# The first layer's shift and scale in two column parts instead of one, in a three-part-precision transformer kernel

## The reference

```python
cond = jax.nn.silu(c)                                   # (1, 1024)
mod = cond @ ada_w[l] + ada_b[l]                        # (1, 3072)
shift, scale, gate = jnp.split(mod, 3, axis=-1)
h = x * (1.0 + scale[:, None, :]) + shift[:, None, :]
proj = h @ w_in                                         # even_mixer: u, v, z_a, x_b, z_b
v = layer_norm(v.reshape(B, S, GMLP_HEADS, GMLP_HEAD_DIM), norm_g, norm_b)
sv = jnp.einsum('hts,bnshd->bnthd', w, v) + bs.T[:, :, None]
```

## Time and profile before

| | us |
|---|---|
| median of 3 runs | 1318.17 (1317.94 to 1319.11) |
| the profiled execution: time | 1319.02 |
| the profiled execution: span | 1317.2 |
| TensorE busy | 1289.7 (98%) |
| VectorE, ScalarE, GpSimd busy | 941.3, 580.2, 357.4 |
| first matmul of any kind | 10.86 |
| first matmul of tile 0 | 34.10 |

### The profile page before, as it was taken

The page is one execution under the profiler, slowest core; times in us unless marked ns, Lnnn a source line. Parts: engine busy times, 40 slices in busy tenths (PEclk is TensorE's granted clock), DMA queues, the critical chain, the costliest instruction groups (busy, mean ns, idle before and its releaser), DMA issues.

```text
span 1317.2 us, 18039 instructions
## 1 busy us (share of the span) xinstructions
PE 1289.7 (98%) x6874; PEld 1106.0 (84%) x6874; DVE 941.3 (71%) x1415; ACT 580.2 (44%) x889; POOL 357.4 (27%) x262
## 2 busy tenths in 40 slices
PE   5999999999999999999999999999999999999997
PEld 5998888778898888888888878888888988888887
DVE  7765654796777558888678888776785577776663
ACT  1422322321264347666422587653452477734441
POOL 1200210055620004655434221122115322221122
PEclk9999999999999999999999999999999999999999
DMA  9565666537725620111234311213533111212111
GB/s 376 171 199 180 187 201 193 158 117 204 234 79 153 174 87 21 41 52 51 88 122 142 112 65 64 96 53 110 154 97 115 65 64 65 95 55 75 64 64 64
DMA packets 35093, 155.18 MB, mean 118 GB/s; under 512 B 6848, under 2 KB 9024, under 8 KB 23744
## 3 DMA queue, kind: packets, MB, share of 16 engines
q1 hardware_dynamic: 35008, 154.04, 36.9%
HBM read 151.92 MB, written 2.10 MB: 117 GB/s over the span
## 4 chain that ended last, share of the span: by engine, by line
PE 88%; DVE 5%; issue 3%; ACT 1%; POOL 1%; DMA 1%; SPq 0%; DVEq 0%; POOLq 0%; ACTq 0%
PE bank L971 25%; PE bank L973 24%; PE bank L972 24%; PE bank L1334 2%; PE bank L1319 1%; PE bank L1338 1%; PE bank L1179 1%; DVE keep L2477 1%; PE bank L1510 1%; PE bank L1537 1%; PE bank L1535 1%; DMA ada_first<-adat 1%; PE bank L1307 1%; PE bank L1306 1%; PE bank L978 1%
## 5 line engine op out<-in xcount | busy, mean ns | idle before, releaser
L971 PE MATMUL bank<-h_lo,w_hi 128*128 128x512 f32 (+1 forms) x1064 | 407.1, 383 | 0.7 <-DVE k_both L2045 0.5
L973 PE MATMUL bank<-h_hi,w_hi 128*128 128x512 f32 (+1 forms) x1064 | 402.5, 378 | 0.0
L972 PE MATMUL bank<-h_hi,w_lo 128*128 128x512 f32 (+1 forms) x1064 | 402.2, 378 | 0.0
L1883 DVE TENSOR_TENSOR w_lo<-w_raw,w_hi 128x2048 fp32r<-128x2048 f32 (+2 forms) x91 | 207.1, 2275 | 75.6 <-ACT w_hi L1557 75.4
L971 PEld LDWEIGHTS bank<-h_lo,w_hi 128*128 128x128 f32 x1064 | 200.2, 188 | 37.6 <-issue 1.8
L973 PEld LDWEIGHTS bank<-h_hi,w_hi 128*128 128x128 f32 x1064 | 200.1, 188 | 37.7
L972 PEld LDWEIGHTS bank<-h_hi,w_lo 128*128 128x128 f32 x1064 | 200.3, 188 | 36.3 <-issue 0.2
L1557 ACT ACTIVATE w_hi<-w_raw 128x2048 fp32r<-128x2048 f32 (+2 forms) x91 | 166.7, 1832 | 89.7 <-PE bank L973 72.9
L1925 DVE SCALAR_TENSOR_TENSOR acc<-ada_raw,cond_four,acc 128x1024 f32<-128x1024 f32 x62 | 87.5, 1411 | 3.9 <-DMA ada_raw<-adat 1.0
L1685 ACT ACTIVATE tmp<-bank 128x512 f32<-128x512 f32 x48 | 28.8, 600 | 112.3 <-PE bank L973 111.1
L2477 DVE TENSOR_TENSOR_SCAN keep<-keep,rmats 128x127 f32<-128x127 f32 (+2 forms) x64 | 57.8, 942 | 1.0
(11 more groups left out here) (359 smaller groups left out, 2688.1 us busy)
## 6 DMA issues: line engine op xcount, KB each, us to landing
w_raw<-wt SPq DMA_DIRECT2D x83, 1024.0 KB, 5.5
ada_raw<-adat SPq DMA_DIRECT2D x256, 128.0 KB, 2.9
ada_first<-adat SPq DMA_DIRECT2D x16, 512.0 KB, 12.2
ada_raw<-adat SPq DMA_DIRECT2D x32, 256.0 KB, 5.7
w_raw<-wt SPq DMA_DIRECT2D x8, 640.0 KB, 3.9
spare_raw<-wt SPq DMA_DIRECT2D x3, 1024.0 KB, 5.1
x<-xt SPq DMA_DIRECT2D x4, 512.0 KB, 15.5
out<-outf SPq DMA_DIRECT2D x16, 128.0 KB, 1.8
```

Source lines behind the costliest of these rows:

```text
L971: pe.matmul(dst, ah, bl, start=start, stop=False, skip_group_check=True)
L972: pe.matmul(dst, al, bh, start=False, stop=False, skip_group_check=True)
L973: return pe.matmul(dst, ah, bh, start=False, stop=stop, skip_group_check=True)
L1883: dve.tensor_tensor(w_lo[wb[T]][:, 0:n], w_raw[wb[T]][:, 0:n], f(w_hi[wb[T]][:, 0:n]), ALU.subtract).then_inc(w_lo_done, 1)
```

## The change

**1. Two column parts.** Features are cut at block 5: part 0 is k = 0 to 4 (columns 0 to 639 of every piece), part 1 is k = 5 to 7 (384 columns). Everything of the opening is loaded and made by part: pieces two at a time (`ada_pair`), tiles 0 and 1 (1280 and 768 columns), x. SP issues all of part 0 with tile 1's first part, and then part 1, tile 0's second part before x's last three blocks.

**2. More direct pieces.** Pieces 1, 3, 5 and 7 of shift and scale in part 0 and of shift in part 1 are direct; scale in part 1 has none.

**3. Start on five blocks.** A new step `first_blocks`: TensorE does blocks 0 to 4 of tile 0's pair, then of tile 1's pair, with the direct pieces and sums of part 1 put in between tile 1's blocks. It then does blocks 5 to 7 of both. The four chunks lie in banks 0 to 3.

**4. Fillers.** Ten 128x197 matmuls on `cols` at the start (`warm_up`), one after each direct piece of shift, two 128x512 after each of scale, five before the first block and four before block 5.

**5. GpSimd** makes the low parts of tiles 0 and 1's columns 1280 to 2047 (before: DVE).

**6. Order.** ACT and DVE split tiles 3 and 4 earlier in their programs (`split_ahead`), and `spatial(0)` to `spatial(3)` stand one tile later.

The diff, cut to its core:

```diff
-DIRECT_PIECES = (1, 3)
+DIRECT_PIECES = {(0, 0): (1, 3, 5, 7), (0, 1): (1, 3, 5, 7), (1, 0): (1, 3, 5, 7), (1, 1): ()}
+FIRST_BLOCKS = 5
+X_PARTS = ((0, 2), (2, 4), (4, 5), (5, 8))
...
     steps.append(dict(op="first_mods"))
-    steps.append(dict(op="h", l=0))
...
+    steps.append(dict(op="h", l=0, part=0))
+    steps.append(dict(op="first_blocks"))
+    steps.append(dict(op="h", l=0, part=1))
+    both = [begin(split=False), begin()]
+    head_pair(0, both[0])
+    split_ahead(3)
+    steps.append(dict(op="spatial_rows"))
+    head_pair(1, both[1])
+    T = begin(split=False)
+    chunk("V", T, h=2, c=0)
+    split_ahead(4)
+    chunk("V", T, h=2, c=1)
+    spatial(0)
...
+            weights(0, 0)
+            for i in range(SEC):
+                ada_pair(i, 0)
...
+            for i in range(3):
+                features(i)
+            weights(1, 0)
+            for i in range(SEC // 2):
+                ada_pair(i, 1)
+            weights(0, 1)
+            features(3)
+            for i in range(SEC // 2, SEC):
+                ada_pair(i, 1)
+            weights(1, 1)
...
                 if before_in[T] >= 0:
                     sp.wait_ge(w_lo_done, before_in[T] + 1)
+                if before_in[T] in range(2):
+                    sp.wait_ge(first_lo, before_in[T] + 1)
...
             def first_mods():
 
+                pe.wait_ge(cols_in, 16)
+                warm_up(10)
                 pe.wait_ge(cond_done, 1)
...
+                for u in range(2):
+                    for k in DIRECT_PIECES[0, u]:
+                        direct_piece(0, u, k)
...
+                        if u == 1:
+                            keep_busy(2, 3)
+                        else:
+                            warm_up(1)
...
+                    first_sums(0, u, 6 + u)
+                keep_busy(5, 3)
...
+            def first_blocks():
+
+                pe.wait_ge(first_lo, 1)
+                chunk_pair(PAIRED[0], FIRST_K[0])
+                pe.wait_ge(first_lo, 2)
+                for k in FIRST_K[0]:
+                    chunk_pair(PAIRED[1], (k,))
+                    for i in DIRECT_PIECES[1, 0][2 * k:2 * k + 2]:
+                        direct_piece(1, 0, i)
+                    if k == FIRST_BLOCKS - 3:
+                        first_sums(1, 0, 6)
+                    if k == FIRST_BLOCKS - 2:
+                        first_sums(1, 1, 7)
+                keep_busy(4, 5)
...
+                elif op == "h" and d["part"] == 0:
+                    first_columns(0)
+                    for k in FIRST_K[0]:
+                        h_low(k)
+                        if 1 <= k < FIRST_BLOCKS:
+                            first_piece(left + k - 1)
...
+                elif op == "first_blocks":
+                    for T in range(2):
+                        c = FIRST_WEIGHTS[1]
+                        pool.wait_ge(w_hi_done, T + 1)
+                        pool.tensor_tensor(w_lo[T][:, c], w_raw[T][:, c], f(w_hi[T][:, c]),
+                                           ALU.subtract).then_inc(w_lo_done, 1)
```

More of the change, by code:

```diff
@@ L217, in border, with head_pair, split_ahead, spatial @@
         steps[-1].update(right)
-    steps.append(dict(op="first_mods"))
-    steps.append(dict(op="h", l=0))
-    for h in range(GH):
-        T = begin()
-        chunk("V", T, h=h, c=0)
-        chunk("V", T, h=h, c=1)
-        if h == 0:
-            steps.append(dict(op="spatial_rows"))
-        else:
-            steps.append(dict(op="spatial", h=h - 1))
-        after_tile(T)
+    def head_pair(h, T):
+        return [chunk("V", T, h=h, c=c) for c in range(2)]
+    def split_ahead(T):
+        steps.append(dict(op="split_ahead", T=T))
+    def spatial(h):
+        steps.append(dict(op="spatial", h=h))
+    steps.append(dict(op="first_mods"))
+    steps.append(dict(op="h", l=0, part=0))
[11 more added lines that the diff above has]
+    spatial(0)
+    after_tile(T)
+    T = begin(split=False)
+    head_pair(3, T)
+    spatial(1)
+    after_tile(T)
     for kind in ("U", "Z", "ZB"):
@@ L236, in plan_steps @@
                           cast=kind == "Z", val=kind == "Z")
[L237 to L238 removed]
+                if kind == "U" and (i, sub) in ((0, 1), (1, 0)):
+                    spatial(2 + i)
             after_tile(T)
@@ L739, in pieces_summed @@
         def pieces_summed(q):
-            return q - sum(i < q for i in DIRECT_PIECES)
+            return q - 2 * SEC
         piece_at = {}
@@ new lines, in first_mods, with warm_up, direct_piece @@
+                keep_busy(5, 3)
+            def warm_up(n):
+                for i in range(n):
+                    pe.matmul(bank[:, 3, 0:NCOL], cols[:, 0:P], cols[:], start=True, stop=True)
+            def direct_piece(part, u, k):
+                pe.wait_ge(ada_first_landed[(SEC * u + k) // 2][part], 16)
+                for j in FIRST_K[part]:
+                    pe.matmul(bank[:, 6 + u, j:j + 1], ada_first[:, SEC * u + k, j * P:(j + 1) * P], cond[:, k:k + 1],
+                              start=k == 1 and j == FIRST_K[part][0], stop=False, skip_group_check=True)
@@ new lines, in first_sums @@
+            def first_sums(part, u, bk):
+                pe.wait_ge(first_sum, first_summed(part, u))
+                own = not DIRECT_PIECES[part, u]
+                for j in FIRST_K[part]:
+                    ins = pe.matmul(bank[:, bk, j:j + 1], acc[:, u, j * P:(j + 1) * P], ones[:, 0:1],
+                                    start=own and j == FIRST_K[part][0], stop=True, skip_group_check=True)
+                ins.then_inc(first_full, 1)
+            def first_blocks():
[11 more added lines that the diff above has]
+                keep_busy(4, 5)
@@ L2347, in _ @@
                     T = d["T"]
-                    if not d["late_low"]:
+                    if d["split"] and not d["late_low"]:
                         for t in split_with(T):
```

200 lines of the change are left out of this document (112 added, 88 removed).

## The result

The changed kernel takes 1335.38 us at the median of six executions (1330.64 to 1341.14), the kernel before 1318.78 us beside it (1317.94 to 1320.94). The ratio is 1.0126 with a 95% interval of 1.0092 to 1.0161: 1.3% slower, where 1315.4 us was forecast. The profiled execution took 1330.99 us, a quick one of the six; what the longer ones add, up to 10 us, is the subject of experiments 9 to 11.

What follows compares the result with a forecast made beforehand. TensorE, busy 98% of the span, bounds the kernel: first block 8.4 us earlier, 5.3 us work added, 3.1 us net gain; 2.2 to 3.1 against the median gave 1315.4 us (own range 1313.6 to 1316.8, overall 1313.4 to 1323.5).

Steps and rivals of the forecast that it cites:

- Take the high level from the ten warm-ups on: Opening, TensorE: clock assumed at 2.4 GHz from the warm-ups on, so a part-0 direct piece costs 1.1 us, not 2.15.
- The first block: End of opening: TensorE starts tile 0's first block at 25.7 us instead of 34.10, 8.4 us earlier.
- The rival that came: Opening: clock falls amid mostly one-column matmuls, first block 32.5, total 1323.4 us (1320.9 to 1327 by extent); chance 0.24.
- low from the third shift piece on: 1327: Longest case of the clock's fall in the opening: low level from shift's third direct piece, total 1327 us.
- The second rival: Hand-over stalls: tile 1's first low part or a part-1 landing 1 to 2 us late, 1316.4 to 1317.4 us; chance 0.11.
- each piece has a filler, a fifth to a third of the time, and TensorE has no long pause: Opening, TensorE: the prediction's argument against the clock falling there.
- the row that spoke against it: Opening of the kernel before: 7 us of one-column matmuls before 17.8 us did not raise the clock.
- The rule that idle gaps throttle the clock: Skill page's rule on TensorE's clock; by it alone the clock's fall would not happen; no row showed it.
- The added work: TensorE, tiles 0 and 1: direct pieces +4.0, four fillers +0.9, changes of matmul kind +0.4, 5.3 us in all.
- The thinnest cover: Tile 1's first low part on DVE ends near 32.9 us; TensorE ends its five blocks at 32.95.
- the 1.9 to 4.7 of the forecast: GpSimd's low parts of 768 columns in tiles 0 and 1: 1.9 to 4.7 us, from earlier subtraction rows.
- Later work: After the opening: later `spatial` and splits stay hidden; rival has 1 to 3 us given back, 1316.4 to 1318.4; chance 0.05.

Runs made afterwards that it cites:

- experiments 9 to 11: The changed kernel unchanged, run three times more: 1329.60 and 1335.24 us; then median 1335.49 us of four; then median 1335.92 us of five.
- experiment 5: Changed kernel with one direct piece each in part 0 of shift and scale, dense 128x512 fillers, GpSimd's low parts on DVE: 1318.81 us, ratio 0.9995.
- experiment 1: Changed kernel with four warm-ups instead of one behind shift's direct pieces and five fillers instead of two behind scale's: 1334.36 us, ratio 1.0111.
- experiment 8: Changed kernel with DVE instead of GpSimd making the low parts of tiles 0 and 1, five executions: 1329.41 us, ratio 1.0077.
- experiment 2: Changed kernel with only pieces 3 and 7 of shift and scale direct in part 0, sixteen warm-ups and dense fillers: 1322.77 us, ratio 1.0031.
- experiment 3: Experiment 2 with one direct piece each in part 0 of shift and scale, none in part 1, and 4, 18, 15 and 8 fillers: 1322.95 us.
- experiment 6: Experiment 5 with the low parts of tiles 0 and 1's columns 1280 to 2047 back on GpSimd: 1319.07 us, ratio 0.9998.
- experiments 7 and 8: Changed kernel with only GpSimd's part undone, DVE making those low parts, run twice: 1329.97 us (four executions) and 1329.41 us (five).
- experiment 4: Changed kernel without any filler or warm-up before the first block, the four before block 5 kept: 1327.12 us, ratio 1.0058.

## Why the prediction was wrong

**The step that failed** is the first of its account of TensorE: "Take the high level from the ten warm-ups on." The clock was high from 6.8 us, as taken, but it fell at 13.63 us, in shift's third direct piece, and everything up to 40.94 us ran at the low level. With this level kept, by dense fillers and fewer direct pieces, the same two-part opening is level with before (experiment 5). More filler alone kept the clock high for 13.7 us more (experiment 1); fewer one-column matmuls and more filler together kept it throughout (experiment 5). The two were not taken apart beyond that, and what mix is just enough is not shown: five fillers a piece held it for 20.5 us and two pieces with eight for 10.2. The forecast's reason for the high level, a filler at each piece and no long pause, does not hold: in experiment 8's trace there was hardly a pause (9.26 of 9.31 us), and the clock fell all the same.

**The first block**, 25.7 forecast, 37.14 measured. The last pair that shift's direct pieces need was forecast for 13.65 and landed at 14.92, since tile 0's part and the first pair came later (8.48 us instead of 7.4) and a pair takes 1.65 us, not 1.6: 1.3 us. The other 10.2 us are the low clock: behind 14.92 the forecast had 12.05 us, the trace has 22.2.

**The rival that came** is the first, the clock's fall in the opening, given 0.24. Its mechanism was right and its price too small. It gave "low from the third shift piece on: 1327", and that was the case that came: 1327 + 1.3 for the landings + 1.6 for the wait is 1329.9, and the profiled execution took 1331.0; 0.85 of the rest is that the 1327 is reckoned against the median of before and not against its profiled execution. The second rival, a stalled hand-over of 1 to 2 us for tile 1's first low part, came with it, at 1.6 us. The forecast sat on "each piece has a filler, a fifth to a third of the time, and TensorE has no long pause"; the row that spoke against it, 7 us of one-column work that didn't raise the clock, was read and then given too little weight. The rule that idle gaps throttle the clock (the Trainium skill, TensorE: Matmul & The Clock Gate, the part on HAM oscillation) was rightly kept out of the sum: gaps aren't needed, for in experiments 1 and 2 the clock fell with TensorE busy in all of the 20.5 and 10.2 us before. That the clock can fall in a wait is seen too, at 44.83 us in experiment 3 (a wait of 3.66 us).

**The added work**, 5.3 us forecast for tiles 0 and 1: right. Experiment 5 has 5.1 to the end of tile 2, in which the changes from one kind of matmul to the other and back are included. In the changed kernel the same stretch takes 83.27 - 37.14 = 46.13 us, 8.9 more than before; 5.1 of added work, the wait of 1.6 and half of the 3.8 us at the low level behind 37.14 make 8.6 of it.

**The thinnest cover** was named rightly, tile 1's first low part, but its price was wrong. The forecast had it end 0.05 us ahead of TensorE's need and counted nothing for GpSimd's subtractions beside it. These lasted 4.39 us for two, 2.2 each, inside the 1.9 to 4.7 of the forecast. But the price was looked for on GpSimd alone, and it fell on DVE: 2.33 and 2.20 us instead of 0.68 and 0.61, which made TensorE wait 1.6 to 1.8 us. The Trainium skill, GPSIMD Engine Reference, section Specifications, says that GpSimd shares its SBUF interfaces with VectorE, with contention for DVE instructions in a 2-port perf mode or with two SBUF inputs. These rows agree for the two-input instructions; the one-input instruction of experiment 6 was stretched too (0.42 to 2.01 us), and no run shows in which mode it ran. The rows also say what sets the size. Each of the four stretched instructions ended 0.2 to 0.6 us behind the end of a subtraction (44.22 and 46.34 us behind 43.66 and 45.92 in the changed kernel, 35.72 and 42.50 behind 35.49 and 42.09 in experiment 6). So each seems to have stood until GpSimd's instruction was done, and the price goes with the length of that instruction, not with DVE's own.

**The median** lies 4.4 us above the profiled execution, which no step of the forecast foresaw: in some executions the clock is low for longer. One trace shows such a fall behind the wait; without GpSimd's part (experiments 7 and 8) none of nine executions is above 1332.6 us, though their two traces have falls of 3.4 us near 372 and 744 us.

**Later work.** Forecast as hidden, and it was: between 130 and 1290 us nothing changed.

## What to carry to other kernels

Before shortening an opening, look at what TensorE's records cost at each end of it, and ask what would keep the granted clock high through the new one. Here one-column matmuls did not, and a filler too thin to hold the clock was worse than none: it ran on the path at half speed. Moving a small task to GpSimd is not free for DVE: for each DVE instruction that can meet it, price up to the whole length of GpSimd's instruction, above all where a thin cover stands behind them.

## What was not expected of the hardware

- The clock fell while TensorE was busy without any gap: after 20.5 us of it in experiment 1 and 10.2 us in experiment 2.
- One-column work didn't raise it either: in experiment 4 TensorE worked 21.6 of the 22.5 us from 8.0 to 30.5 us, all of it one-column matmuls, and was still low behind it, up to 35.86.
- Falls of 3.4 us came in the middle of full tiles, near 375 and 745 us, in some executions of kernels with and without the change.
- Two-input DVE instructions beside a GpSimd subtraction took 2.33 us for 512 columns instead of 0.69 and 2.20 us for 384 instead of 0.61; a one-input one 2.01 instead of 0.42; each ended shortly behind the subtraction.
- One kernel, unchanged, took 1329.6 to 1341.8 us from execution to execution, with the mean clock going from 0.989 to 0.978; the same kernel with GpSimd's low parts on DVE stayed within 1327.9 to 1332.6.
